# Dense products of a two-layer block: single plain four-byte matmuls in place of three split ones

## The reference

```
h   = x + hybrid_mixer(rmsnorm(x))         # layer 1, mixer
        proj = hn @ w_in                   # 1024 x (1024 z + 1536 xbc + 16 dt + 3*1024 short conv)
        SSD (Mamba-2 scan, 16 heads) on xbc, dt;  gated by silu(z), group norm
        sc = sc_b * conv3(sc_c * sc_v), group norm
        concat(ssd_out, sc_out) @ w_out    # 2048 x 1024
h   = h + hierarchical_moe(rmsnorm(h))     # 32 experts, top 2 of a group; w_gate, w_up, w_down: 6 MB each expert
h   = rmsnorm(h)
h   = h + mixer_2(rms_norm(h))             # RG-LRU and gated linear attention
        w_in_2: 1024 x 2576, w_out_2: 1024 x 1024
h   = h + ffn_2(rms_norm(h))               # w_ffn_in_2: 1024 x (2 x 2816), w_ffn_out_2: 2816 x 1024
out = rms_norm(h)
```

## Time and profile before

| | us |
|---|---|
| runs of the kernel before: median of 3 | 1002.63 |
| lowest and highest | 1001.35, 1002.91 |
| the profiled run, its own time | 1001.36 |
| its span, first to last instruction | 999.6 |
| TensorE busy | 798.0 (80%) |
| DVE, ACT, POOL busy | 450.3, 315.4, 89.2 |
| moved by DMA | 287 MB |

### The profile page before, as it was taken

How to read it: one execution, slowest core, us unless ns; L and a number is a source line. 1 busy time by engine, 2 the same in 40 slices (tenths; PEclk the granted TensorE clock), 3 DMA queues, 4 the chain that set the end, 5 groups by cost and what they waited for, 6 DMA issues and landing times.

```text
span 999.6 us, 16237 instructions
## 1 busy us (share of the span) xinstructions
PE 798.0 (80%) x6842; PEld 619.9 (62%) x6842; DVE 450.3 (45%) x779; ACT 315.4 (32%) x513; POOL 89.2 (9%) x111
## 2 busy tenths in 40 slices
PE   6999999998946484656746466577998999999996
PEld 6978898775624243333413334244887799999994
DVE  5855849555322031312203122126647665555555
ACT  6754355632100000000000000004484454444443
POOL 1019554100000000000000000000001010000000
PEclk9999999999978687879869798799999999999998
DMA  9974334358999999999999999999653546544101
GB/s 304 322 273 169 114 140 168 142 203 348 379 427 425 428 427 428 427 426 425 426 427 428 427 426 427 428 424 384 252 168 105 187 168 201 198 175 169 43 1 43
DMA packets 70775, 287.04 MB, mean 287 GB/s; under 512 B 11521, under 2 KB 36398, under 8 KB 58414
## 3 DMA queue, kind: packets, MB, share of 16 engines
q1 hardware_dynamic: 70386, 285.38, 72.2%
q10 hardware_dynamic: 316, 0.58, 0.2%
HBM read 284.90 MB, written 1.05 MB: 286 GB/s over the span
## 4 chain that ended last, share of the span: by engine, by line
DMA 36%; PE 33%; issue 22%; DVE 4%; ACT 3%; POOL 2%; SPq 0%; POOLq 0%; ACTq 0%; DVEq 0%
DMA down_a<-in_w_down_dram 29%; PE bank L575 12%; PE bank L608 5%; PE bank L2044 4%; DMA pair_d<-in_w_up_dram 4%; PE bank L587 3%; DMA ring<-in_w_down_dram 2%; PE bank L2027 2%; PE bank L2017 1%; PE bank L1875 1%; PE bank L596 1%; DVE act_p L522 1%; ACT w_hi L550 1%; DVE w_lo L560 1%; POOL seg_r L841 1%
## 5 line engine op out<-in xcount | busy, mean ns | idle before, releaser
L575 PE MATMUL bank<-act_p,w_hi 128*128 128x256 f32 x1440 | 266.8, 287 | 7.7 <-issue 7.6
L560 DVE TENSOR_TENSOR w_lo<-ring,w_hi 128x1024 fp32r<-128x1024 f32 x137 | 177.2, 1294 | 145.6 <-ACT w_hi L550 145.2
L575 PEld LDWEIGHTS bank<-act_p,w_hi 128*128 128x128 f32 x1440 | 226.5, 193 | 11.7 <-issue 11.3
L550 ACT ACTIVATE w_hi<-ring 128x1024 fp32r<-128x1024 f32 x138 | 145.9, 1058 | 187.1 <-PE bank L575 130.3
L575 PE MATMUL bank<-act_p,w_lo 128*128 128x256 f32 x720 | 204.7, 284 | 0.0
L575 PEld LDWEIGHTS bank<-act_p,w_lo 128*128 128x128 f32 x720 | 139.1, 193 | 0.0
L1591 DVE COPY y_e<-bank 32x256 f32<-32x256 f32 x64 | 27.2, 424 | 238.9 <-PE bank L2044 238.5
L1099 ACT ACTIVATE y_e<-bank 32x256 f32<-32x256 f32 x64 | 23.9, 374 | 283.2 <-PE bank L2044 282.9
L2027 PE MATMUL bank<-ring,x_t 128*32 128x256 f32 x1536 | 94.9, 402 | 8.2 <-issue 7.4
L2044 PE MATMUL bank<-down_a,h_t 128*32 128x256 f32 x512 | 42.3, 487 | 70.3 <-DMA down_a<-in_w_down_dram 58.7
L608 PE MATMUL bank<-w_hi,act_q 128*128 128x512 f32 x304 | 95.3, 395 | 0.4 <-issue 0.4
(11 more groups left out here) (350 smaller groups left out, 923.4 us busy)
## 6 DMA issues: line engine op xcount, KB each, us to landing
ring<-in_w_up_dram SPq DMA_DIRECT2D x24, 2048.0 KB, 34.8
ring<-in_w_gate_dram SPq DMA_DIRECT2D x24, 2048.0 KB, 30.4
down_a<-in_w_down_dram SPq DMA_DIRECT2D x16, 2048.0 KB, 26.1
ring<-in_w_in_dram SPq DMA_DIRECT2D x15, 2048.0 KB, 18.9
down_b<-in_w_down_dram SPq DMA_DIRECT2D x15, 2048.0 KB, 26.1
ring<-in_w_ffn_in_dram SPq DMA_DIRECT2D x22, 1024.0 KB, 6.8
pair_d<-in_w_gate_dram SPq DMA_DIRECT2D x8, 2048.0 KB, 30.5
pair_d<-in_w_up_dram SPq DMA_DIRECT2D x8, 2048.0 KB, 34.9
```

The lines of the kernel that those rows point to most:

```text
L550: nc.scalar.activation(parts(w_hi, g, view), view, ACT.Copy).then_inc(split_hi, 1)
L560: engine.tensor_tensor(parts(w_lo, g, view), view, h, ALU.subtract).then_inc(split_lo, 1)
L575: mm = nc.tensor.matmul(dst, parts(wt, g, grans[g][1])[:, k, :], a[:, x_part, k, :], start=(k == 0 and i == 0), stop=(k == KC - 1 and i == 2))
```

## The change

- The types: `act_p`, `act_q`, `m_gt` and `seg_r` are plain float32 with no second part; `w_hi`, `w_lo`, `ws_hi`, `ws_lo`, `sc_f`, `adt_r` are gone, and with them `hi`, `lo`, and the splits of all activations.
- `turn_gran`, `flow_gran`, `row_gran` and `narrow_gran` read the weights in the ring slot (or `w_dt`, `w_z`) and do one matmul where there were three. TensorE waits for the unit's landing itself. A ring slot is freed by `gran_used`, not by the splits.
- `turn_act` and `turn_dve` share the chunks, even and odd, and work side by side.
- The gains go into the activations: `norm_sc` multiplies by `sc_norm`, `keep_ssd` (in place of `hi_ssd` and `lo_ssd`) by `ssd_norm`.
- `seg` is one matmul; `seg_r` has two buffers. `xdt` and `mask_seg` move from POOL to DVE.
- The narrow product for dt moves from behind granule 11 to granule 8, the turning of dt from granule 13 to 10, `dt_start` and the exponential on ACT two granules and one forward.
- In the FFN the gated product is written into `act_q` by DVE directly.
- Loads: the up half of expert 3 is issued behind unit 9 and the down weights of expert 1 behind unit 11, where both stood behind granule 59. `down_b` and the up half of `pair_d` have memory of their own.

```diff
     ring = sb("ring", [P, SLOTS, UNIT])
-    with ExitStack() as same:
-        down_b = sb("down_b", [P, UNIT], where=same)
-    w_hi = sb("w_hi", [P, 2, GR], F32R)
-    w_lo = sb("w_lo", [P, 2, GR], F32R)
+    down_b = sb("down_b", [P, UNIT])
     with ExitStack() as same:
         pair_d = sb("pair_d", [P, 2, UNIT], where=same)
-    act_p = sb("act_p", [P, 2, KC, T], F32R)
-    with ExitStack() as same:
-        act_q = sb("act_q", [P, 2, KC, T], F32R, where=same)
-    sc_f = sb("sc_f", [P, 2, KC, T])
+    act_p = sb("act_p", [P, KC, T])
+    act_q = sb("act_q", [P, KC, T])
+    sb("pair_d_up", [P, UNIT])
...
     def turn_act(act, t, gain):
-        for c in range(KC):
+        for c in range(0, KC, 2):
             act.wait_ge(turned, KC * t + c + 1)
-            nc.scalar.activation(act_p[:, 0, c, :], bank[TURN_BANK[t][c]][:, 0:T], ACT.Copy,
-                                 scale=pcol(gain, c)).then_inc(turn_hi, 1)
+            nc.scalar.activation(act_p[:, c, :], bank[TURN_BANK[t][c]][:, 0:T], ACT.Copy,
+                                 scale=pcol(gain, c)).then_inc(turn_even, 1)
...
     def turn_gran(pe, g, dst, a, t=None):
 
-        pe.wait_ge(split_lo, g + 1)
-        pe.wait_ge(split_hi, g + 1)
+        landed_wait(pe, g)
         for k in range(KC):
             if t is not None:
-                pe.wait_ge(turn_lo, KC * t + k + 1)
-            for i, (wt, x_part) in enumerate(PASSES):
-                mm = nc.tensor.matmul(dst, parts(wt, g, grans[g][1])[:, k, :], a[:, x_part, k, :],
-                                      start=(k == 0 and i == 0), stop=(k == KC - 1 and i == 2))
+                pe.wait_ge((turn_even, turn_odd)[k % 2], KC // 2 * t + k // 2 + 1)
+            mm = nc.tensor.matmul(dst, grans[g][1][:, k, :], a[:, k, :], start=(k == 0), stop=(k == KC - 1))
         mm.then_inc(gran_used, 1)
...
     def row_gran(pe, g, banks, a_chunk, first, last, free=None, pieces=BY_BLOCK):
 
-        pe.wait_ge(split_lo, g + 1)
-        pe.wait_ge(split_hi, g + 1)
+        landed_wait(pe, g)
         for n, (b, half) in enumerate(pieces):
             if free is not None:
                 pe.wait_ge(free[0], free[1] + 2 * b + half)
-            for i, (wt, x_part) in enumerate(PASSES):
-                mm = nc.tensor.matmul(banks[2 * b + half][:, :], a_chunk[:, x_part, b * P:(b + 1) * P],
-                                      wt[:, g % 2, half * 512:(half + 1) * 512],
-                                      start=(first and i == 0), stop=(last and i == 2))
+            mm = nc.tensor.matmul(banks[2 * b + half][:, :], a_chunk[:, b * P:(b + 1) * P],
+                                  grans[g][1][:, half * 512:(half + 1) * 512], start=first, stop=last)
...
         for u in range(UA):
             if u >= SLOTS:
-                sp.wait_ge(split_hi, last_gran[u - SLOTS] + 1)
-                sp.wait_ge(split_lo, last_gran[u - SLOTS] + 1)
+                sp.wait_ge(gran_used, last_gran[u - SLOTS] + 1)
...
+            if u == 9:
+                load_half(3, 1, 3)
+            if u == 11:
+                load_down(1, 1)
...
         sp.wait_ge(gran_used, GA)
         load_half(3, 0, 3)
-        load_half(3, 1, 3)
-        load_down(1, 1)
         sp.wait_ge(routed, 1)
         load_down(0, 0)
...
-            for n in range(2):
-                mm = nc.tensor.matmul(bank[5][:, :], m_gt[:, :],
-                                      seg_r[:, n, :, :].rearrange("p h l -> p (h l)"), start=(n == 0), stop=(n == 1))
-            mm.then_inc(seg_raw, 1)
+            nc.tensor.matmul(bank[5][:, :], m_gt[:, :], seg_r[:, it % 2, :, :].rearrange("p h l -> p (h l)"),
+                             start=True, stop=True).then_inc(seg_raw, 1)
...
+            if g in (G_SC, G_SC + 2):
+                xdt_block((g - G_SC) // 2)
+            if G_SC + 4 <= g < G_SC + 20 and (g - G_SC) % 2 == 0:
+                mask_seg((g - G_SC - 4) // 2)
...
                 if g == GU[f] + 3:
                     dve.wait_ge(f_silu, f + 1)
-                    nc.vector.tensor_tensor(lx[:, f % 4, :], lx[:, f % 4, :], gate_bank(f)[:, T:2 * T],
+                    if f >= 8:
+                        dve.wait_ge(gran_used, GO[f - 8] + 1)
+                    nc.vector.tensor_tensor(act_q[:, f % 8, :], lx[:, f % 4, :], gate_bank(f)[:, T:2 * T],
                                             ALU.mult).then_inc(f_prod, 1)
```

More of the change, by code:

```diff
@@ L224, in flow_grans, with row_grans @@
         for k in range(0, KC, kn):
[L225 to L233, removed]
+            grans.append((u, whole(u).rearrange("p (k n) -> p k n", k=KC)[:, k:k + kn, c0:c0 + n]))
+    def row_grans(u, n):
+        for j in range(n):
+            grans.append((u, whole(u)[:, j * GR:(j + 1) * GR]))
     def pcol(name, i):
@@ L513, in turn_act @@
     def turn_act(act, t, gain):
-        for c in range(KC):
+        for c in range(0, KC, 2):
             act.wait_ge(turned, KC * t + c + 1)
-            nc.scalar.activation(act_p[:, 0, c, :], bank[TURN_BANK[t][c]][:, 0:T], ACT.Copy,
-                                 scale=pcol(gain, c)).then_inc(turn_hi, 1)
+            nc.scalar.activation(act_p[:, c, :], bank[TURN_BANK[t][c]][:, 0:T], ACT.Copy,
+                                 scale=pcol(gain, c)).then_inc(turn_even, 1)
     def turn_dve(dve, t, gain):
[L520 to L530, removed]
+        for c in range(1, KC, 2):
+            dve.wait_ge(turned, KC * t + c + 1)
+            nc.vector.tensor_scalar(act_p[:, c, :], bank[TURN_BANK[t][c]][:, 0:T], pcol(gain, c), None,
+                                    ALU.mult).then_inc(turn_odd, 1)
     def landed_wait(eng, g):
@@ L542, in unit_landed @@
         return landed_c[u % SLOTS], 16 * PARTS_OF[u]
[L544 to L562, removed]
-                                           op0=ALU.mult, op1=ALU.subtract).then_inc(split_lo, 1)
@@ L577, in turn_gran @@
         mm.then_inc(gran_used, 1)
     def flow_gran(pe, g, dsts, a, k0):
-        pe.wait_ge(split_lo, g + 1)
-        pe.wait_ge(split_hi, g + 1)
-        kn = grans[g][1].shape[1]
-        for k in range(kn):
+        landed_wait(pe, g)
+        view = grans[g][1]
+        for k in range(view.shape[1]):
             for b in range(TB):
-                for i, (wt, x_part) in enumerate(PASSES):
-                    mm = nc.tensor.matmul(dsts[b], a[:, x_part, k0 + k, b * P:(b + 1) * P],
-                                          parts(wt, g, grans[g][1])[:, k, :],
-                                          start=(k0 + k == 0 and i == 0), stop=(k0 + k == KC - 1 and i == 2))
+                mm = nc.tensor.matmul(dsts[b], a[:, k0 + k, b * P:(b + 1) * P], view[:, k, :],
+                                      start=(k0 + k == 0), stop=(k0 + k == KC - 1))
@@ L590, in flow_gran, with narrow_gran @@
         mm.then_inc(gran_used, 1)
-    def narrow_gran(pe, dst):
+    def narrow_gran(pe, dst, wt):
         for k in range(KC):
-            for i, (wt, x_part) in enumerate(((ws_hi, 0), (ws_hi, 1), (ws_lo, 0))):
-                mm = nc.tensor.matmul(dst, wt[:, k, :], act_p[:, x_part, k, :], start=(k == 0 and i == 0),
-                                      stop=(k == KC - 1 and i == 2))
+            mm = nc.tensor.matmul(dst, wt[:, k, :], act_p[:, k, :], start=(k == 0), stop=(k == KC - 1))
         return mm
@@ L1123, in _ @@
         nc.scalar.activation(y_e[:, :], tok[:, 0, :], ACT.Square, accum_out=sm[:, 74:75]).then_inc(ss_act, 1)
-        for g in range(GA, GA + 2):
-            hi(act, g)
         act.wait_ge(rstd_ready, 3)
         nc.scalar.activation(nrm[:, 1, :], tok[:, 1, :], ACT.Copy, scale=sm[:, 83:84]).then_inc(nrm_act, 1)
-        nc.scalar.activation(ws_hi[:, :, :], w_z[:, :, :], ACT.Copy).then_inc(narrow_hi, 1)
         turn_act(act, 1, "norm1_2")
@@ L1644, in _ @@
         turn_dve(dve, 1, "norm1_2")
-        lo(dve, GA + 1)
         for b in range(TB):
```

318 lines of the change are left out of this document (109 added, 209 removed).

## The result

The changed kernel took **1074.97 us** (median, 1072.52 to 1081.64) where the kernel before took 1002.77 in the same comparison: a ratio of 1.0723, 95% interval 1.0663 to 1.0784. The change makes the kernel slower by 7%. The profiled execution took 1077.14 us with a span of 1075.4, so the traces differ by 75.8 us of span.

What follows compares the result with a forecast made beforehand. TensorE was taken to bound both mixers and the FFN, DMA the experts. Mixer +29.0, preloads 0, layer 2's mixer +10.1, turn -0.9, FFN +40.7, end -0.4 sum to +78.5: 1079.9 us profiled, 1081 median, range 1070 to 1093.

Steps and rivals of the forecast that it cites:

- The price of a granule: Dense products: a granule rises from 2.88 to 3.46 us (256 columns) and from 2.7475 to 3.44 us (512).
- The page's rule: Dense products: true FP32 takes four passes, so time becomes 4/3; as a rival, 1130 us, chance 3%.
- FFN: +40.7 predicted: FFN stretch: 44 granules of 256 columns and 22 of 512 go from 187.2 to 227.9 us, no idle time to regain.
- Mixer: work +41.4 predicted: First mixer: dearer granules, narrow dt product and `seg` add 41.4 us of TensorE work; with fewer stalls, +29.0 us net.
- the rest that I left, 2 us: First mixer: of 14.4 us of stalls, 2 us were assumed to stay, giving -12.4 us.
- `mask_seg` and `xdt` on DVE at nothing: Mixer: moving these from POOL to DVE costs nothing; without cover, `mask_seg` costs up to 0.7 us eight times.
- The preloads at 0, with -9.8 as the other end: Mixer to experts: loading 4.19 MB earlier gains 0 us, since no step there waits for a load; alternatively -9.8 us.
- Layer 2's mixer: +10.1 predicted: Layer 2's mixer: +18.8 us of work, less 8.7 us of the 10.7 us of stalls, 2 us left: +10.1 us.
- the forecast's own case: Whole kernel: 1076 to 1086 us, with residual stalls of 0 to about 9 us; chance 70%.
- the preload case: Rival at the experts: their stream is DMA-bound from the mixer's end, so 9.8 us come off: 1071 us, chance 8%.
- the stall case: Rival: stalls stay or others replace them; half or all of 25 us remain instead of 4: 1090 to 1102 us, 13%.
- the last four rivals: Dense work: four passes, 1130 us, 3%; lower FFN clock, 1104, 2%; faster plain matmuls, 835 at best, 2%; three-part matmuls, 980, 2%.

Runs made afterwards that it cites:

- the run without splits: Kernel before with its three split matmuls per product, weights split only for each layer's first two granules (stale afterwards), activations still split: 978.49 us, ratio 0.9759.
- after: The first profile of the changed kernel, unedited: profiled execution 1077.14 us, span 1075.4 us.
- the reordered kernel: Kernel before with `ws_lo` moved ahead of `turn_dve` in layer 2, scaled product and step-size copy one granule later, products and splits unchanged: 997.50 us, ratio 0.9956.

## Why the prediction was right, and where its terms were off

**The price of a granule** was predicted at 3.46 and 3.44 us, from plain matmuls on other tiles. Measured are 3.46 and 3.43. The step that carried the whole forecast was to price the new operation by rows that have its form, and not by counting. It held on work 130 times as long as the rows.

The page's rule, four passes in the place of three (the Trainium skill, "FP8 and Floating Point Precision", section TensorE Precision Notes), would make each granule 1.33 times as long. The trace gives 3.46 / 2.88 = 1.20 and 3.43 / 2.7475 = 1.25: the rule had the sign right and the size not.

**FFN: +40.7 predicted, +39.54 measured.** The new stretch, 227.9 predicted, is 228.1. The step that was off by 1.2 us is "187.2 us, which is the whole stretch, so there is no idle time to win back": the stretch was 188.56, and the run without splits brought it to 187.35. The 1.2 us were delays between matmuls, too short to show as idle time, and they went.

**Mixer: work +41.4 predicted, 41.1 measured** between two kernels that don't wait. The stalls were put at 14.4 us by subtraction and measured at 13.6. The term that was mis-sized is the rest that I left, 2 us: TensorE is busy in every microsecond of the stretch, so nothing was left, and the stretch grew by 27.5 instead of 29.0. The cause was only half told. The prediction says that the change takes the late splits away; with all splits kept, the longer granule took away some 10 us of the 13.6 by itself. The prediction names the longer granule, 3.46 in place of 2.88, only beside it.

**`mask_seg` and `xdt` on DVE at nothing:** right. Behind the fourth granule the mixer takes 221.87 us with either engine. Their own lengths were put too low, 0.7 and 1.2 us where they take 0.80 and 1.64, and that had no effect.

**The preloads at 0, with -9.8 as the other end:** right, and shown by the run with the loads put back. The argument, that the queue is idle anyway before the routing releases the next loads, is visible as a window at 426 GB/s in one kernel and empty in the other, with the same time. DMA idles in the changed kernel from about 260 us to 270, about the 10 us and more that the prediction named. The experts' stretch was 427.0 to 429.0 us in the profiles of the changed kernel and 428.3 with the preloads put back, against 430.05 to 430.3 in before and in the runs made from it with split matmuls, and 429.7 in the one with plain matmuls and all splits. So something of the change other than the preloads may have taken off 1 to 2 us there; its cause stays open.

**Layer 2's mixer: +10.1 predicted, +9.05 measured;** here too nothing of the 2 us left for stalls was left. Stalls and slow clock were put at 10.7 us and measured at 9.3 (5.4 and the 3.9 that the run without splits keeps), the work at 18.8 and 18.4. The turn gave -1.3 instead of -0.9, the tail -0.35 instead of -0.4.

**The sum.** 1079.9 us predicted for the profiled run, 1077.14 measured. The three dense stages came out 3.7 us below the forecast together, the experts' stretch gave 1.15 more, and the closing's lower clock took back 2.58. The step from there to the median, +1.3, went the wrong way: it was the distance in the kernel before, and such a distance isn't a property that a change keeps. The median of 1074.97 us lies in the stated range, but 1 us below the forecast's own case (1076 to 1086), in the part that was taken in for the preload case, and not by that cause: the preloads brought nothing, and the same kernel's second median is 1076.82, so the single runs' spread of several us is the likelier reason, which isn't shown. One sum on the chances is off: outside 1070 to 1093 lie half of the stall case and the last four rivals, 15.5% and not 13%.

**The rivals.** That stalls stay or move is refuted by the first row of after: no wait of TensorE stands in the three stretches. The clock stayed at 1.00 through 228 us of plain matmuls. Of the case that the kernel gets faster the prediction said that it decides at 0.388 us per plain matmul of 256 columns; it is 0.4325, so the plain form couldn't win. What the stalls were worth at all is seen in the run without splits: 24 us by the medians, 21.7 between the two profiles. The dearer work was 41.1 us in the mixer, 40.75 in the FFN and, with the 2.55 us of idleness and the 1.4 of the slow narrow product taken off that run, 110.19 - 91.8 = 18.4 in layer 2's mixer (18.8 predicted): 100 us.

## What to carry to other kernels

When an edit trades cheap instructions on a bound engine for fewer dear ones, price the new form from rows of the same form in the old trace, and set against it the stalls that the bound engine really has: here 100 us of new work against 24 of stalls. Splitting work on DVE and ACT cost nothing here where it kept pace (in the FFN DVE was busy for 107 us with all splits and 23 without them, and both stretches are 228.1 us); a relief that they get reaches the end only through a wait of the bound engine. The Trainium skill, "Perfetto Trace Analysis", section Optimization Strategies, says to relieve the engines for which TensorE waits; the reordered kernel did that alone and got 0.4%, while the change did it too and paid four times as much for it as it could bring.

## What the runs showed of the hardware that was not expected

- Work that is only there to keep TensorE from rest can get onto the path that sets the end. Five idle matmuls of 512 columns took 4.54 us at a granted clock of 1.00, and 6.26 us on the chain where it was partly 0.50. The stretch around them took 30.16 and 34.18 us, of which the routing products at the lower level cost 3.1 us and the idle matmuls about 1. Which of the two an execution gets varied between profiles of nearly the same kernel (30.15 to 30.20 us in eight, 32.51 in one, 34.17 and 34.18 in two).
- The lower level followed soon after a rest of 2.0 to 2.5 us in three places: the granule of the earlier trace rows, the narrow product of layer 2 (4.11 us for 2.74, behind 2.03 us of waiting, in the run without splits too), and the idle matmuls behind the rank product. It did not follow in every execution: behind a rest of 2.46 us the reordered kernel with three idle matmuls stayed at 1.00.
- In the closing of the experts and the first granule of layer 2, the lower level moved from one to the other: 5.72 and 3.46 us in one profile of the changed kernel, 3.90 and 4.63 with the loads put back, and in neither place in the changed kernel's second profile (3.90 and 3.46).
- The plain matmul's period, 0.216 us a record at 256 columns and 0.429 at 512, was the same over the FFN as over 1.7 us: 44 x 3.46 + 22 x 3.43 = 227.7 of its 228.1 us.
